# Matmul slabs set inside the delta rounds and the fourth attention, leading queries of four tiles taken as one pair, and two steps of the first two attentions reordered

## The chip, the cores and the metric

The kernel runs on one core of a Trainium2 chip. The metric is the device time in microseconds, the median of several executions. TensorE (PE) does the matmuls, VectorE (DVE), ScalarE (ACT) and GpSimd (POOL) the elementwise work, SyncE (SP) issues the DMAs.

## The reference

Four transformer layers on x (1024 features, 512 tokens). The first two belong to one model (attention with ALiBi, then neighbourhood attention, each with a cross-attention into 256 memory tokens). The last two belong to another, which sets 16 meta tokens ahead of the 512: a layer with a short convolution and a gated delta rule, and a layer with windowed attention. Each layer ends in a gated feed-forward part.

```python
# third layer
y_a = a_gate_out * causal_dwconv(a_gate_in * a_h, conv_a_w)      # the gate: 4 slabs of a_gate_out
o = gated_delta_rule(q, k, v, beta, g)                           # 4 heads, chunks of tokens
y = concat([y_a, rms_norm(o) * silu(z)]) @ w_out
# fourth layer: 16 query heads, 4 key heads, 64 features each
q, k = rms_norm(h @ wq) * d ** -0.5, rms_norm(h @ wk); v = h @ wv
pm = sink_softmax(causal(qm @ km.T), sink); om = pm @ vm         # the 16 leading (meta) queries
p = sink_softmax([qb @ km.T, banded(qb @ kband.T)], sink)        # four blocks of 128 queries
y = concat([om, p @ [vm, vband]]) @ wo
```

## The kernel before

**Slabs.** Every weight comes in slabs of 128 output features by 1024 inputs (`UP` = 8 blocks) or 1408. SP loads a slab into `raw[:, s]` (s = 0 or 1), ACT rounds it to `w_hi` (L818, `split_hi`, two halves), POOL makes `w_lo` (L606, `split_lo`, two halves). TensorE multiplies each block three times (hi·hi, hi·lo, lo·hi) by the activations, in two column halves of 264: 48 matmuls for a slab on all 528 tokens. The slot s of `w_hi` is free again when `pe_done` counts the slab before last; the accumulator `acc(s)` (PSUM banks 0, 1 or 2, 3) when DVE has read it (`acc_free[s]`). Each engine runs its own queue in the order written, and semaphores hold them together.

**First two attentions (`attend_tiles`).** Eight tiles (two heads each) of four pairs (128 queries by 256, 384 or 512 keys; tiles 6 and 7 are the memory heads). At step p TensorE does `scores(p)` (L1363), `turn(p-2)` (transposes of the probabilities, L1472) and `values(p-3)` (L1373); at the first step of a tile also `reciprocals(tile-2)` (L1490), which waits for `inv_ready` (DVE's `invert`: reciprocal and the copy L1771) and for `y_moved` (ACT's `move_y`, L1002, a copy of the tile's output out of the bank that the reciprocals then overwrite). ACT's step is `turned(p-1, h)` (L993) and `probs(p, h)` (L910) for two heads; then `y_hi(tile-2)` at pair 2 of a tile and `move_y(tile-1)` at pair 3. DVE's step is `biased` twice (L1786), `invert(tile-1)` at pair 0 and `normalise(tile-2)` at pair 1.

**Third layer.** The stage `even` ends with four slabs, the gate slabs (q0+12, q0+13; s = 0, 1), whose results DVE multiplies into `conv_y`. The stage `delta` follows: rounds -1 to 6 of five pieces i = 0 to 4. In a round, chunk r runs its levels (`first_product`, `second_products`), chunk r-1 its `tail`, chunk r+1 its `pre` work, chunk r-2 its `head`. Chunk 0 has 16 tokens, the others 128. `pre` uses banks 0 and 1, `second_products` writes bank 6. Eight slab parts of `out` stand at the end of `delta` (`slab_part`).

**Fourth attention (`attend`).** Eight tiles of five pairs: pair 0 holds the 16 leading queries, pairs 1 to 4 the four blocks of 128. Six slabs of the projection (`Hidden`, tiles 2 to 7 of q) lie in it: tile T (0 to 5) carries slab T in pairs 1, 2 and 3 (18, 18 and 12 matmuls, L1419), ahead of `values` in each step. DVE's `scaled` reads it at pair 3, ACT squares it at pair 4 (L939), TensorE sums the squares at pair 0 of the next tile (the mean square, L1406, in the same banks 4 and 5), ACT takes the logarithm and the exponential there (L944, L947), and DVE normalises at pair 1. A step p of the other work: TensorE `scores(p)` (L1363), `turn_both(p-2)` (L1396), `values(p-3)` (L1373) with the transposed reciprocals (L1437) at its end; in tiles 6 and 7 also two products of ones that nothing reads (L1435). ACT: `probs(p, 0)`, `turned_both(p-1)` (L923, L926), `probs(p, 1)`, `move_y(p-2)` (L953, waits for L1437), `y_hi(p-3)` (L958). DVE: sink column and `biased` (p), `invert(p-1)`, `normalise(p-3)` (L1761 on `y_sb`), for which `turn_both` of the next step waits. POOL stages q, k and v of each tile and makes `y_lo`. Then the stage `out` runs its 8 slabs.

Of the kernel before, what the change touches and what calls it, by code (L numbers as in the profile page):

```python
# [43 lines left out]
MIXED = 6  # L44
HEAD_TILES = (8, 9, 0, 1)
# [31 lines left out]
def plan():  # L77
# [25 lines left out]
    def att(**kw):  # L103
        add("att", **kw)
        c["pair"] += kw["nt"] * len(kw["blocks"])
        c["tile"] += kw["nt"]
        c["unit"] += kw["nt"] * len(kw["blocks"])
# [7 lines left out]
    def tail(gain, blk, layer, conv, following, mixed=False):  # L115
# [7 lines left out]
        for _ in range(FF_G):  # L123
# [15 lines left out]
    s_blocks = [dict(q=0, nq=META, keys=[(P, META)], chunks=[(0, META, 4)], bias="meta"),  # L139
                dict(q=META, nq=P, keys=[(0, KEY_STEP)], chunks=[(0, P, 0), (P, META, 4)], bias="first")]  # L140
    for b in range(1, 4):
        s_blocks.append(dict(q=META + P * b, nq=P, keys=[(KEY_STEP * (b - 1), P + KEY_STEP)],
                             chunks=[(0, P, b - 1), (KEY_STEP, P, b), (P, META, 4)], bias="band"))

# [72 lines left out]
def build(nc, d):  # L217
# [6 lines left out]
    with ctx:  # L224
# [18 lines left out]
        meta_mask = cst[0:META, o + 3 * P + 2 * META:o + 3 * P + 3 * META]  # L243
# [9 lines left out]
        neg_rows = sb("neg_rows", [P, 28])  # L253
        neg_sinks = [neg_rows[:, 0:12], neg_rows[:, 12:28]]
# [26 lines left out]
        small = region("small", 14464)  # L281
# [34 lines left out]
        v_st = small("v_st", [P, 2, 5, P])  # L316
        sq = small("sq", [P, 2, TOK], f32, 7400)
# [54 lines left out]
        def quad(k, n):  # L372

            return ps[:, k * BANK:k * BANK + DN_H * n].rearrange("p (h n) -> p h n", h=DN_H)

# [49 lines left out]
        class Chunk:  # L425

            def __init__(self, c):
                self.c, (self.t0, self.n) = c, CHUNKS[c]
                self.tok = slice(self.t0, self.t0 + self.n)
                self.levels = levels_of(c)  # L430
                self.a_t, self.x_m, self.x_t = a_ts[c % 2], x_ms[c % 2], x_ts[c % 2]
                self.state, self.next_state = states[c % 2], states[(c + 1) % 2]
                self.top, self.final = min(self.n, P // 2), "vn" if c else "vt"
                self.out_bank, self.ms_bank = 4 if c == LAST else 3, 2 if c < LAST - 1 else 5
                self.qk_t, self.erow = qk_ts[c % 3], erows[c % 3]
                self.elast = elasts[:, c % 3, :]
                self.sq4 = (slice(0, self.n), slice(None), slice(0, self.n))

            def after(self, engine, part, maker, name):

                engine.wait_ge(d_sem[part, maker], dn_at[part, maker, self.c, name])

        def rounds():

            for r in range(-1, len(CHUNKS) + 2):
                for i in range(PIECES):
# [5 lines left out]
                    yield here, mid, old, new, fin, i  # L452

        class Pair:

            def __init__(self, st, g, pos):
                self.st, self.g, self.pos = st, g, pos
                nb = len(st.blocks)  # L460
                self.b, self.slot, self.tile_slot = pos % nb, pos % 2, pos // nb
                self.c = st.blocks[self.b]
                self.nq, self.n = self.c["nq"], sum(n for _, n in self.c["keys"])
                self.tile = 2 * g + pos // nb
                self.nth = g * (2 * nb) + pos
                self.count, self.unit = self.nth + st.pair0, self.nth + st.unit0
                self.exists = self.nth >= 0
                self.q = slice(self.c["q"], self.c["q"] + self.nq)
                self.full = sum(1 for ch in self.c["chunks"] if ch[1] == P)
                self.halves = [(2 * self.nth + h) % 3 for h in range(2)]  # L470
                self.inv = (slice(0, self.nq), self.nth // 4 % 2, self.nth % 4, slice(None))

            def back(self, k):
                n = 2 * len(self.st.blocks)
                return Pair(self.st, self.g, self.pos - k) if self.pos >= k else Pair(self.st, self.g - 1, self.pos - k + n)

        def over_pairs(st, body):

            for g in range(st.nt // 2):
                for pos in range(2 * len(st.blocks)):  # L480
                    body(Pair(st, g, pos))
# [42 lines left out]
        def last_pair(st):  # L524
            return Pair(st, st.nt // 2 - 1, 2 * len(st.blocks) - 1)
# [74 lines left out]
        def _(pool):  # L600
# [32 lines left out]
            def attend(st):  # L633

                nb = len(st.blocks)
                hi_y, lo_y = outputs(st)

                def stage_q(i):
                    pool.wait_ge(s_done, (i - 1) * nb + st.pair0)
                    pool.wait_ge(tn_out, st.tn0 if i < 2 else st.tn0 + i - 1)  # L640
                    split(q_hi[:, i % 2, :], q_lo[:, i % 2, :], qk[st.h][:, st.qt + i, :], 2 * (i + st.tile0) + 2)\
                        .then_inc(qk_staged, 1)

                def stage_k(i):
                    pool.wait_ge(s_done, (i - 1) * nb + st.pair0)
                    at = i // st.group + st.kt
                    keys = qk[st.h][:, at, META:TOK].rearrange("p (b n) -> p b n", n=P)
                    meta = qk[st.h][:, at, 0:META].unsqueeze(1).to_broadcast([P, 4, META])
                    hi, lo = (k[:, i % 2, :].rearrange("p (b n) -> p b n", n=KEY_STEP) for k in (k_hi, k_lo))
                    nc.gpsimd.tensor_copy(hi[:, :, P:KEY_STEP], meta)  # L650
                    nc.gpsimd.tensor_copy(hi[:, :, 0:P], keys).then_inc(hi_staged, 1)
                    pool.wait_ge(hi_staged, 2 * (i + st.tile0) + 1)
# [3 lines left out]
                def stage_v(i):  # L656
                    pool.wait_ge(pv_done, (i - 1) * nb + st.pair0)
                    f = bass.ds((i // st.group) * P, P)
                    nc.gpsimd.tensor_copy(v_st[:, i % 2, 0:4, :], val_m[st.h][:, 0:4, f])
                    nc.gpsimd.tensor_copy(v_st[0:META, i % 2, 4, :], val_m[st.h][0:META, 4, f]).then_inc(v_staged, 1)  # L660

                def y_lo(i, b):
                    c = st.blocks[b]
                    q = slice(c["q"], c["q"] + c["nq"])
                    k = i * nb + b
                    pool.wait_ge(y_hi_ready, k + st.unit0 + 1)
                    nc.gpsimd.tensor_tensor(lo_y[:, st.y + i, q], y_sb[st.h][:, k % 2, 0:c["nq"]],
                                            hi_y[:, st.y + i, q].bitcast(f32), ALU.subtract).then_inc(y_lo_ready, 1)
                chores = [stage_k, stage_v, stage_q]
# [6 lines left out]
                for i in range(1, st.nt + 1):  # L676
                    more = Hidden(st, i) if 2 <= i < MIXED + 2 else None
                    for b in range(nb):
                        if b < 3 and i < st.nt:
                            chores[b](i)  # L680
                        if b >= 3 and more:
                            split_lo(more.q, more.s, UP, (b - 3,))
                        if b >= 3:
                            y_lo(i - 1, b - 3)
                        elif i >= 2:
                            y_lo(i - 2, b - 3 + nb)
                for b in range(nb - 3, nb):
                    y_lo(st.nt - 1, b)
# [59 lines left out]
            def delta(st):  # L748
# [8 lines left out]
                for here, mid, old, new, fin, i in rounds():  # L757
# [27 lines left out]
                    if new and i == 4:  # L785
# [4 lines left out]
                        over_heads(new.x_t[new.sq4], all_heads(ident, n), new.x_t[new.sq4], ALU.subtract, "pre")  # L790
                    if mid and mid.c == LAST and i == 2:
                        stream(st.slab0 + 2)

            for n, st in enumerate(stages):
                if st.kind == "delta":
                    stream(st.slab0)
# [11 lines left out]
        def _(act):  # L808
# [104 lines left out]
            def attend(st):  # L913

                def probs(p, h):
                    s_h = s_sb[0:p.nq, p.slot, h, 0:p.n + 1]
                    exponentials(p, h, s_h, s_h, -1.0, p_sum[p.inv][:, h:h + 1])

                def turned_both(p):
                    act.wait_ge(pt_done, 2 * p.count + 2)  # L920
                    act.wait_ge(pv_done, p.count - 1)
                    if p.full:
                        nc.scalar.activation(p_t[:, p.slot, :, 0:p.full, 0:p.nq],  # L923
                                             bank(3).rearrange("p (h c n) -> p h c n", h=2, n=P)[:, :, 0:p.full, 0:p.nq],
                                             ACT.Copy)
                    nc.scalar.activation(p_t[0:META, p.slot, :, p.full, 0:p.nq],  # L926
                                         bank(6 + p.slot)[0:META, 2 * P:4 * P].rearrange("p (h n) -> p h n", h=2)[:, :, 0:p.nq],
                                         ACT.Copy).then_inc(pt_ready[0], 1)

                def split_hidden(p):  # L930
                    if p.b in (2, 3) and 2 <= p.tile + 1 < MIXED + 2:
                        w = Hidden(st, p.tile + 1)
                        split_hi(w.q, w.s, UP, (p.b - 2,))

                def hidden(p):
                    if p.b == 4 and p.tile < MIXED:
# [3 lines left out]
                    if p.b == 0 and 0 <= p.tile - 1 < MIXED:  # L940
                        w = Hidden(st, p.tile - 1)
# [8 lines left out]
                def move_y(p):  # L950
                    act.wait_ge(pv_done, p.count + 1)
                    act.wait_ge(y_lo_ready, p.unit - 1)
                    nc.scalar.activation(y_sb[st.h][:, p.slot, 0:p.nq], bank(6 + p.slot)[:, 0:p.nq], ACT.Copy)\  # L953
                        .then_inc(y_moved, 1)

                def y_hi(p):
                    act.wait_ge(y_ready, p.unit + 1)
                    nc.scalar.activation(outputs(st)[0][:, st.y + p.tile, p.q], y_sb[st.h][:, p.slot, 0:p.nq],  # L958
                                         ACT.Copy).then_inc(y_hi_ready, 1)

                def step(p):
                    probs(p, 0)
                    hidden(p)
                    if p.back(1).exists:
                        turned_both(p.back(1))
                    probs(p, 1)
                    if p.back(2).exists:
                        move_y(p.back(2))
                    if p.back(3).exists:
                        y_hi(p.back(3))  # L970
                    split_hidden(p)
# [9 lines left out]
            def attend_tiles(st):  # L981
# [27 lines left out]
                def step(p):  # L1009
# [1372 lines left out]
```

## Time and profile before

| | us |
|---|---|
| median of 3 runs | 2696.24 (2682.99 to 2702.41) |
| the profiled execution, its own time | 2692.25 |
| its span, first to last instruction | 2690.4 |
| first attention | about 120 to 204 |
| second attention | about 742 to 854 |
| gate slabs, then delta rounds | 1423.7 to 1447.2, then to 1621.9 |
| fourth attention, its end | 2083.3 to 2265.8 |

The profile is of one execution. TensorE's busy share is high because ends of pipelined matmuls are modelled; what counts is where it waits, and at which clock it ran (PEclk: 1.00 is 2.4 GHz, 0.50 is 1.2 GHz).

### The profile page before, as it was taken

What the parts mean: (1) busy time and instruction counts of PE and PEld (TensorE: products, weight loads), DVE (VectorE), ACT (ScalarE), POOL (GpSimd) and SP (SyncE); (2) the same over time, 40 slices, a digit from 0 to 9 for tenths busy, and PEclk for the clock granted to TensorE, in tenths of its full rate; (3) what the DMA queues carried; (4) which work ended last, traced back from release to release, by engine and by line L of the source; (5) the groups of instructions that cost most, each with busy time, mean ns of one, the idle gap of its engine ahead of it and who ended that gap; (6) DMA issues with size and microseconds to landing.
All of it is one profiled execution on the core that took longest, in us unless ns stands there. A gap on an engine that the chain in (4) does not pass through costs nothing.

```text
span 2690.4 us, 45550 instructions
## 1 busy us (share of the span) xinstructions
PE 2582.8 (96%) x16250; PEld 2238.3 (83%) x16250; DVE 938.9 (35%) x1675; ACT 938.4 (35%) x1974; POOL 1180.5 (44%) x964
## 2 busy tenths in 40 slices
PE   7989999999988999999998989999999889999999
PEld 7757888888866888888997879999999667998897
DVE  3253221222153321226652444432432553442341
ACT  4274222232275322234342233222233563332231
POOL 4544444444543444444443434444444442444443
PEclk9999999999998999999997899999999897999999
DMA  4211232232320223232221002222222100223222
GB/s 166 82 34 64 93 104 88 96 108 87 107 71 17 94 94 102 86 102 95 84 79 40 1 17 87 86 96 84 93 93 73 32 25 24 87 92 102 86 99 96
DMA packets 60231, 212.89 MB, mean 79 GB/s; under 512 B 8544, under 2 KB 11232, under 8 KB 60128
## 3 DMA queue, kind: packets, MB, share of 16 engines
q1 hardware_dynamic: 60128, 211.53, 23.6%
q8 instruction: 63, 1.03, 0.2%
q14 instruction: 40, 0.33, 0.0%
HBM read 209.41 MB, written 2.10 MB: 79 GB/s over the span
## 4 chain that ended last, share of the span: by engine, by line
PE 91%; DVE 3%; ACT 3%; issue 2%; DMA 0%; DVEq 0%; POOL 0%; ACTq 0%; SPq 0%; POOLq 0%
PE ps L1249 76%; PE ps L1575 3%; PE ps L1373 2%; PE ps L1363 2%; ACT s_sb L910 1%; PE ps L1472 1%; PE ps L1419 1%; PE ps L1396 1%; PE ps L1264 1%; DVE s_sb L1786 1%; PE ps L1435 0%; DVE s_sb L1761 0%; PE ps L1490 0%; PE ps L1566 0%; ACT p_t L993 0%
## 5 line engine op out<-in xcount | busy, mean ns | idle before, releaser
L606 POOL TENSOR_TENSOR w_lo<-raw,w_hi 128x512 fp32r<-128x512 f32 (+1 forms) x704 | 976.5, 1408 | 1165.1 <-ACT w_hi L818 1164.7
L818 ACT ACTIVATE w_hi<-raw 128x512 fp32r<-128x512 f32 (+1 forms) x704 | 426.9, 653 | 1324.3 <-PE ps L1249 1302.1
L1249 PE MATMUL ps<-h_hi,w_hi 128*128 128x264 f32 (+2 forms) x2960 | 845.4, 332 | 0.1
L1249 PE MATMUL ps<-h_lo,w_hi 128*128 128x264 f32 (+2 forms) x2960 | 844.0, 332 | 0.0
L1249 PE MATMUL ps<-h_hi,w_lo 128*128 128x264 f32 (+2 forms) x2960 | 841.9, 331 | 0.0
L1249 PEld LDWEIGHTS ps<-h_hi,w_hi 128*128 128x128 f32 x2960 | 503.7, 188 | 60.1 <-issue 1.6
L1249 PEld LDWEIGHTS ps<-h_hi,w_lo 128*128 128x128 f32 x2960 | 500.5, 188 | 53.9
L1249 PEld LDWEIGHTS ps<-h_lo,w_hi 128*128 128x128 f32 x2960 | 499.7, 188 | 54.8 <-issue 1.0
L1249 PE MATMUL ps<-act_lo,w_hi 128*128 128x512 f32 (+1 forms) x880 | 280.5, 351 | 0.0
L1249 PE MATMUL ps<-act_hi,w_lo 128*128 128x512 f32 (+1 forms) x880 | 279.8, 350 | 0.0
L1249 PE MATMUL ps<-act_hi,w_hi 128*128 128x512 f32 (+1 forms) x880 | 278.8, 349 | 0.0
L1761 DVE TENSOR_TENSOR x<-x,ps 128x512 f32<-128x512 f32 (+3 forms) x96 | 66.5, 693 | 427.5 <-PE ps L1249 423.3
L1249 PEld LDWEIGHTS ps<-act_lo,w_hi 128*128 128x128 f32 x880 | 153.6, 188 | 24.0
L1249 PEld LDWEIGHTS ps<-act_hi,w_hi 128*128 128x128 f32 x880 | 153.3, 188 | 24.3
L1249 PEld LDWEIGHTS ps<-act_hi,w_lo 128*128 128x128 f32 x880 | 153.9, 188 | 22.7
L1761 DVE TENSOR_TENSOR ps<-gated,ps 128x512 f32<-128x512 f32 (+1 forms) x88 | 61.6, 701 | 168.0 <-PE ps L1249 167.7
L1756 DVE SCALAR_TENSOR_TENSOR ps<-padded,vec,ps 128x528 f32<-128x528 f32 (+1 forms) x132 | 101.2, 766 | 27.3 <-issue 16.8
L910 ACT ACTIVATE s_sb<-s_sb,n_max 128x512 f32<-128x512 f32 (+5 forms) x176 | 96.9, 550 | 12.1 <-DVE n_max L1786 12.0
L1761 DVE TENSOR_TENSOR act_lo<-ps,act_hi 128x512 f32 (+1 forms) x88 | 61.2, 696 | 104.3 <-ACT act_hi L1045 104.3
L1373 PE MATMUL ps<-p_t,v_st 128*64 128x128 f32 (+1 forms) x1136 | 95.8, 298 | 0.1
L1761 DVE TENSOR_TENSOR padded<-ps,rstd 128x528 f32<-128x528 f32 (+1 forms) x56 | 39.4, 703 | 153.9 <-PE ps L1249 142.8
L1042 ACT ACTIVATE ps<-ps 128x512 f32<-128x512 f32 (+1 forms) x88 | 51.4, 584 | 107.1 <-DVE ps L1756 107.1
(269 smaller groups left out, 2543.0 us busy)
## 6 DMA issues: line engine op xcount, KB each, us to landing
raw<-slabs_d SPq DMA_DIRECT2D x288, 512.0 KB, 3.3
raw<-slabs_d SPq DMA_DIRECT2D x64, 704.0 KB, 4.0
bias_sb<-rpb_d SPq DMA_DIRECT2D x6, 896.0 KB, 5.2
bias_sb<-alibi_d SPq DMA_DIRECT2D x6, 384.0 KB, 3.2
x<-x_d SPq DMA_DIRECT2D x1, 2048.0 KB, 13.1
out_d<-x SPq DMA_DIRECT2D x8, 256.0 KB, 4.5
mem_in<-mem_d SPq DMA_DIRECT2D x1, 1024.0 KB, 7.2
dn_cst<-dn_consts_d SPq DMA_DIRECT2D x1, 512.0 KB, 4.6
```

Source lines behind the costliest of these rows:

```text
L606: nc.gpsimd.tensor_tensor(w_lo[:, s, a * P:b * P], raw[:, s, a * P:b * P], w_hi[:, s, a * P:b * P].bitcast(f32), ALU.subtract).then_inc(lo ...
L818: nc.scalar.activation(w_hi[:, s, a * P:b * P], raw[:, s, a * P:b * P], ACT.Copy)\
L910: nc.scalar.activation(out, src, ACT.Exp, bias=n_max[0:out.shape[0], p.slot, h:h + 1], scale=sign, accum_out=total).then_inc(p_ready, 1)
L1042: nc.scalar.activation(acc(2, st.used), acc(2, st.used), ACT.Silu).then_inc(silu_ready, 1)
L1249: last = nc.tensor.matmul(ps[:, s * 2 * BANK + po:s * 2 * BANK + po + n], w[:, s, wk], a[:, k, to:to + n], start=(k == 0 and w is w_hi and ...
L1264: last = nc.tensor.matmul(out, a[:, k, t0:t0 + n], w[:, s, wk], start=(k == 0 and w is w_hi and a is hi), stop=(k == DT - 1 and w is w_lo))
L1363: last = nc.tensor.matmul(bank(p.halves[h])[0:p.c["nq"], col:col + n], a[hp, p.tile_slot, p.q], b[hp, p.tile_slot, k0:k0 + n], start=(b is ...
L1373: last = nc.tensor.matmul(out[HD * h:HD * h + HD, :], v_st[0:n, p.tile_slot, vb, HD * h:HD * h + HD], p_t[0:n, p.slot, h, j, 0:p.c["nq"]], ...
L1396: last = nc.tensor.transpose(to, s_sb[0:p.nq, p.slot, h, 1 + col:1 + col + n], ident[0:p.nq, 0:p.nq])
L1575: last = nc.tensor.matmul(out[:, h, :], lhs(h), rhs(h), start=True, stop=True)
L1756: return nc.vector.scalar_tensor_tensor(*a, **kw)
L1761: return nc.vector.tensor_tensor(*a, **kw)
```

## The change

**First two attentions:** ACT's `move_y` goes from pair 3 to pair 2 and `y_hi` from pair 2 to pair 3; DVE's `invert` from pair 0 to pair 2.

**Delta:** of the four gate slabs only the first stays in `even`. The other three lie in the rounds, in parts (`GATE_PARTS`), ahead of `second_products`. `pre` takes banks 6 and 7 for chunks 0 and 1, and chunk 0's `second_products` bank 1. `pre`'s two products of round piece 1 and 2 both stand at piece 2, ACT's first exponentials at piece 1. ACT and POOL split the later slabs inside the rounds.

**Fourth attention:** a list `ORDER` of 34 pairs takes the place of 8 times 5: pairs 0 to 3 of each tile, and two pairs (tile, 4), which hold the leading queries of four tiles (4 times 32 rows of a staged copy `qm_hi`), one after (3, 3), one after (7, 0). k and v are staged once per group of four tiles. The slab of a tile lies in pairs 0, 1, 2 (12, 18, 18 matmuls), at pair 0 behind `values`; squares at pair 2's and logarithm at pair 3's end of ACT's step, the mean square at the end of TensorE's step at pair 3 of the same tile. The first slab of `out` is begun at pairs (6, 0), (6, 2), (7, 0), (7, 2), six matmuls each, and ended behind the last pair (24).

```diff
+ORDER = [(t, b) for t in range(TILES) for b in range(4)]
+ORDER.insert(ORDER.index((7, 0)) + 1, (7, 4))
+ORDER.insert(ORDER.index((3, 3)) + 1, (3, 4))
+FIRST_OUT = {(6, 0): 0, (6, 2): 1, (7, 0): 2, (7, 2): 3}
+        GATE_PARTS = {(-1, 0): (12, 1, range(4)), (-1, 1): (12, 1, range(4, 8)), (-1, 2): (13, 0, range(3)),
+                      (-1, 3): (13, 0, range(3, 6)), (-1, 4): (13, 0, range(6, 8)), (0, 0): (13, 1, range(3)),
+                      (0, 1): (13, 1, range(3, 6)), (0, 2): (13, 1, range(6, 8))}
 # POOL, delta
+                    if r == -1 and i in (0, 3):
+                        split_lo(st.slab0 // 2 - 1, i // 3, UP)
 # ACT, attend: at the end of a step
+                def hidden(p):
+                    if p.b in (0, 1) and 2 <= p.tile + 1 < MIXED + 2:
+                        split_hi(w.q, w.s, UP, (p.b,))
+                    if p.b == 2 and p.tile < MIXED:
                         nc.scalar.activation(head_sq[:, w.s, :], qk[st.h][:, w.tile, :], ACT.Square)
+                    if p.b == 3 and p.tile < MIXED:
                         act.wait_ge(tn_ms, w.tn + 1)
                         nc.scalar.activation(halves_of(head_root[:, w.s, :], 2), split_acc, ACT.Ln, ...)
 # ACT, attend_tiles
-                    if p.b == 3 and p.after(4):
+                    if p.b == 2 and p.after(4):
                         move_y(p.tile - 1, 1 - p.tile_slot)
-                    if p.b == 2 and p.after(8):
+                    if p.b == 3 and p.after(8):
                         y_hi(p.tile - 2, p.tile_slot)
 # ACT, end of even and delta
-                for i in (13, 14):
-                    for s in range(RING):
-                        split_hi(q0 + i, s)
+                split_hi(q0 + 13, 0)
+                early_hi = {(-1, 2): (q0 - 1, 1), (0, 1): (q0, 0), (0, 4): (q0, 1)}
 # TensorE, attend
                 def step(p):
                     scores(p)
+                    if p.nth >= 2:
                         turn_both(p.back(2))
-                    hidden(p)
+                    if p.b:
+                        hidden(p)
+                    if p.nth >= 3:
                         values(p.back(3))
+                    if p.b == 0:
+                        hidden(p)
+                    mean_square(p)
+                    if (p.tile, p.b) in FIRST_OUT:
+                        first_out(st, FIRST_OUT[p.tile, p.b])
 ...
+                pe.wait_ge(y_lo_ready, st.unit0 + len(ORDER))
+                for k in range(4, DT):
+                    first_out(st, k)
+            def first_out(st, k):
+                q, (hi, lo) = (st.slab0 + MIXED) // 2, outputs(st)
+                if k == 0:
+                    begin(q, 0)
+                    pe.wait_ge(tn_rt, st.tn0 + MIXED)
+                if k < 4:
+                    pe.wait_ge(y_lo_ready, st.unit0 + ORDER.index((3, 4)) + 1)
 # TensorE, end of even, delta, out
-                many(q0 + 12, 2, 2, hi, lo)
+                slab(q0 + 12, 0, 2, hi, lo)
+                    if (r, i) in GATE_PARTS:
+                        q, s, parts = GATE_PARTS[r, i]
+                        for k in parts:
+                            slab_part(st, st.slab0 // 2 - 14 + q, s, k)
-                    many(q0, DT // 2, st.blk, *outputs(st))
+                    slab(q0, 1, st.blk, *outputs(st))
+                    many(q0 + 1, DT // 2 - 1, st.blk, *outputs(st))
 # DVE, attend_tiles
-                        if p.b == 0 and p.tile >= 1:
+                        if p.b == 2 and p.tile >= 1:
                             invert(p.tile - 1, 1 - p.tile_slot)
 # DVE, delta
+                gates = {(-1, 2): 1, (0, 0): 2, (0, 3): 3}
```

## Rows read from the trace of the kernel before

**Rows 1.** The page: the span, and the chain that ended last by engine.
```profile
span 2690.4 us, 45550 instructions
...
PE 91%; DVE 3%; ACT 3%; issue 2%; DMA 0%; DVEq 0%; POOL 0%; ACTq 0%; SPq 0%; POOLq 0%
```

**Rows 2.** L1490's waits in 140:172, 172:204, 765:800, 800:856 us (total, times).
```profile
  ACT y_tile L1002: 4.1, 3
...
  ACT y_tile L1002: 3.6, 3
...
  ACT y_tile L1002: 5.1, 3
...
  ACT y_tile L1002: 6.4, 5
```

**Rows 3.** Stretches of one tile: us, busy of PE, PEld, DVE, ACT, POOL, clock.
```profile
153.02:163.67 10.65, 9.07 (x89) 6.38 (x89) 6.45 (x24) 8.27 (x26) 5.61 (x7) 1.00 0.16 47
...
795.51:809.61 14.10, 12.41 (x124) 9.21 (x125) 7.67 (x20) 10.90 (x26) 5.86 (x7) 1.00 0.18 75
```

**Rows 4.** Chain of waits, second attention: start, us, what.
```profile
780.78 0.50 ACT y_tile L1002
...
781.41 0.63 PE ps L1490 x4
```

**Rows 5.** Timeline: DVE's copy of `invert` in each of the two attentions.
```profile
152.70 0.44 DVE L1771 COPY p_rec<-p_inv 128x512 f32<-128x512 f32 x1
...
781.09 1.18 DVE L1771 COPY p_rec<-p_inv 128x512 f32<-128x512 f32 x1
```

**Rows 6.** Chain of waits, gate slabs and delta rounds -1 and 0.
```profile
1423.69 23.48 PE ps L1249 x192
...
1454.50 0.39 PE ps L1575 x8
...
1465.74 1.06 PE ps L1580 x4
...
1470.10 1.24 POOL a_lv L752
...
1472.07 2.05 PE ps L1575 x8
```

**Rows 7.** A stretch of the delta rounds, columns as in rows 3.
```profile
1455.70:1478.20 22.50, 16.22 (x106) 12.99 (x103) 4.04 (x11) 4.46 (x10) 6.94 (x7) 0.50 0.00 1
```

**Rows 8.** Chain of waits, a tile of the fourth attention.
```profile
2165.53 0.86 PE ps L1396 x6
...
2169.30 0.85 PE ps L1396 x6
2170.14 0.89 PE ps L1406 x4
2171.04 0.95 PE ps L1373 x12
```

**Rows 9.** Timeline of ScalarE there.
```profile
2166.41 0.60 ACT L923 ACTIVATE p_t<-ps 128x512 f32<-128x512 f32 x1 [0.40 <-PE ps L1396]
...
2167.68 0.25 ACT L953 ACTIVATE y_sb<-ps 128x128 f32<-128x128 f32 x1
...
2168.96 0.63 ACT L939 ACTIVATE head_sq<-qk 128x528 f32<-128x528 f32 x1
...
2172.46 0.30 ACT L958 ACTIVATE ym_hi<-y_sb 128x128 fp32r<-128x128 f32 x1
...
2172.95 0.68 ACT L944 ACTIVATE head_root<-ps,vec 128x528 f32<-128x528 f32 x1
```

**Rows 10.** Fourth attention: tile 2, tile 5, then tiles 6 and 7 before the drain.
```profile
2126.25:2149.45 23.20, 20.71 (x161) 15.88 (x160) 11.20 (x42) 12.65 (x44) 9.56 (x15) 0.85 0.07 24
...
2190.81:2211.47 20.66, 17.88 (x160) 13.79 (x160) 10.51 (x42) 12.54 (x44) 9.59 (x15) 1.00 0.08 27
2211.47:2251.54 40.07, 37.04 (x216) 25.03 (x215) 16.21 (x73) 19.70 (x74) 11.33 (x19) 0.59 0.08 28
```

More of the change, by code:

```diff
@@ L316, in build @@
         v_st = small("v_st", [P, 2, 5, P])
+        qm_hi, qm_lo = (small(n, [P, TILES, META_Q], f32r) for n in ("qm_hi", "qm_lo"))
         sq = small("sq", [P, 2, TOK], f32, 7400)
@@ L477, in over_pairs, with into, y @@
+            def into(self, t):
+                if self.meta:
+                    return t[:, self.st.y + 4 * self.group:self.st.y + 4 * self.group + 4, 0:META]
+                return t[:, self.st.y + self.tile, self.q]
+            def y(self):
+                y = y_sb[self.st.h][:, self.slot, :]
+                return y.rearrange("p (t n) -> p t n", n=META_Q)[:, :, 0:META] if self.meta else y
         def over_pairs(st, body):
-            for g in range(st.nt // 2):
-                for pos in range(2 * len(st.blocks)):
-                    body(Pair(st, g, pos))
+            for nth in range(len(ORDER)):
+                body(Pair(st, nth))
@@ L675, in attend, with step @@
                 stream(st.slab0 + 2)
[L676 to L688, printed above, removed]
+                def step(p):
+                    more = Hidden(st, p.tile + 1) if 2 <= p.tile + 1 < MIXED + 2 else None
+                    if p.tile == 2 and p.b == 0:
+                        stage_k(1)
+                    if p.tile == 2 and p.b == 2:
+                        stage_v(1)
+                    if p.b == 1 and p.tile + 1 < TILES:
+                        stage_q(p.tile + 1)
+                    if p.b in (2, 3) and more:
+                        split_lo(more.q, more.s, UP, (p.b - 2,))
+                    if p.nth >= 3:
+                        y_lo(p.back(3))
+                over_pairs(st, step)
+                for k in (2, 1, 0):
+                    y_lo(last_pair(st).back(k))
                 streamed(st.slab0 + MIXED + 2)
@@ L755, in all_heads @@
                     return m[0:n, 0:n].unsqueeze(1).to_broadcast([n, DN_H, n])
-                for here, mid, old, new, fin, i in rounds():
+                for r, here, mid, old, new, fin, i in rounds():
                     if here:
@@ L1677, in pre @@
                         k.after(pe, "pre", "pool", "xt")
-                        turn(quad(1, n)[0:n], lambda h: k.x_t[0:n, h, 0:n], n).then_inc(done, 1)
-                for s in range(RING):
-                    pe.wait_ge(acc_free[s], st.slab0 // 2)
-                for here, mid, old, new, fin, i in rounds():
+                        turn(quad(k.pre1, n)[0:n], lambda h: k.x_t[0:n, h, 0:n], n).then_inc(done, 1)
+                for r, here, mid, old, new, fin, i in rounds():
+                    if r == 1 and i == 0:
+                        for s in range(RING):
+                            pe.wait_ge(acc_free[s], st.slab0 // 2)
                     if here:
@@ L1970, in step @@
                         stt(tile, tile, q_gain, head_root[:, w.s, :], ALU.mult, ALU.mult).then_inc(tn_out, 1)
+                for t in range(4):
+                    rows = slice(META_Q * t, META_Q * t + META_Q)
+                    copy(meta_sinks[rows, :, :],
+                         neg_sinks[1][rows, :].rearrange("p (g t h) -> p g t h", g=2, h=2)[:, :, t, :])
                 over_pairs(st, step)
@@ L2238, in delta @@
                 ts(neg_ident[:, :], ident, -1.0, None, ALU.mult).then_inc(gate_made, 1)
-                for here, mid, old, new, fin, i in rounds():
+                gates = {(-1, 2): 1, (0, 0): 2, (0, 3): 3}
+                for r, here, mid, old, new, fin, i in rounds():
+                    if (r, i) in gates:
+                        second_gate(st.slab0 - 4, gates[r, i])
                     if here:
```

315 lines of the change are left out of this document (166 added, 149 removed).

## The prediction

> **What bounds the kernel now.** The page comes first: the chain that ended last runs on TensorE for 91% of a span of 2690.4 us [rows 1]. So time is won only where TensorE waits, runs at the lower clock, or does less. I looked for such places with the page's slices, then took the chain of waits and the busy time by stretch for the three stages that the change touches.
>
> In the first two attentions TensorE stands still once in each tile, ahead of L1490, until ScalarE has moved a tile's output: 4.1 us for three tiles, then 3.6, 5.1 for three, and 6.4 for five [rows 2], 19.2 us for fourteen. In a tile of the second attention that is plain: the move starts at 780.78, at the end of ScalarE's pair 3 [rows 4], and TensorE had come to L1490 well before. ScalarE itself is busy 8.27 of 10.65 us in a tile of the first attention and 10.90 of 14.10 in one of the second [rows 3].
>
> Between the gate slabs and round 1 of delta TensorE has little to do and long chains to wait for. The four gate slabs take 23.48 us from 1423.69 on, and round 1 begins at 1472.07 [rows 6]: 24.9 us for two rounds of small products, most of them at the 1.2 GHz level, where the stretch 1455.7 to 1478.2 stands [rows 7].
>
> In the fourth attention a tile of five pairs takes 20.66 us, one with part of its time at the lower clock 23.20, and tiles 6 and 7, which carry no slab, 40.07 for nine steps at a mean clock of 0.59 [rows 10]. A step without a slab takes 3.77 us from one turn to the next (2165.53 to 2169.30), though TensorE's own work in it is less: it waits for VectorE's biases, reciprocals and normalising [rows 8].
>
> **The change, part by part.**
>
> *A, move_y a pair sooner.* It removes or adds no instruction. The move's input is there: the last values of tile T-1 are made in TensorE's step (T, 2), and ScalarE's step (T, 2) ends a step later, since it needs TensorE's turn of (T, 3). The move then ends one step (about 2.7 to 2.9 us) sooner, more than any wait of 1.2 to 1.7 us, so the wait goes. Twelve of the sixteen waits lie in the loops; from rows 2 they are 7.7 in the first attention, 5.1 for three of the second, and about 3.9 for its last three: 16.7 us. What is late next: ScalarE. In the second attention it has 14.10 - 10.90 = 3.2 us free in a tile, and 1.6 when the tile shrinks by 1.6, so the gain is nearly whole: 6 times 1.4 = 8.4. In the first it has 2.4 free, 1.1 after a shrink of 1.3, and it trades values with TensorE twice in a pair; I take 1.0 of 1.3, 6.0 in all. `invert` moves to pair 2, where TensorE no longer stands still while VectorE makes it: 0.2 + 1.18 us in the second attention [rows 5]. VectorE's step there is 1.75 us of biases, so 3.1 against a step of 2.94; 0.2 us late, which ScalarE's buffer (it takes the maxima half a microsecond after they are there) hides. If it doesn't, 12 times 0.2 = 2.4 are lost; I take half. A: 8.4 + 6.0 - 1.2 = 13. Bounds: 17 (all waits gone), 4 (ScalarE sets the tile, and only a third goes).
>
> The copy of `invert` takes 0.44 us in one attention and 1.18 in the other, where GpSimd's split of q runs beside it [rows 5]. The Trainium skill (GPSIMD Engine Reference, section 1, Specifications) says that GpSimd shares its SBUF interfaces with VectorE, with contention when VectorE's instruction runs in a two-port mode or has two SBUF inputs. By it the copy stays slow wherever it meets a staging, and `y_hi` a pair later pushes GpSimd's staging a pair later too, to just where `invert` now stands. Were the whole 0.74 us on the path in every tile of both attentions, A would be 4 rather than 13; the later bias has the slack named above, so I don't take it.
>
> *B, three gate slabs into the rounds.* Each is 23.48 / 4 = 5.87 us [rows 6], work that stays. Before, from the end of the first gate slab (1423.69 + 5.87 = 1429.56) to round 1: 1472.07 - 1429.56 = 42.5 us. After: round -1 holds two slabs (11.7) and its own small products (2.1 us, an estimate: some twenty of 16 tokens); the chain of chunk 0 (gate row, differences, exponentials, a, its turn) took at most 7.3 us alone, from the slabs' end at 1447.17 to round 0 at 1454.50 [rows 6], and fits between the parts. I add 0.7 for the last wait, for x_m. Round 0: one slab (5.9), its own products, some 6 us at 2.4 GHz (an estimate: what is left of 1472.07 - 1454.50 = 17.6 without the 5.3 below is 12.3 us of products at 1.2 GHz [rows 7] and short waits), and 0.5 for a_m. What stays is the chain behind the last turn, with no slab part beside it: from 1466.80 (end of the turn at 1465.74) to 1472.07, ACT's copy, GpSimd's three products of 1.24 to 1.26 each [rows 6], 5.3 us. Sum 14.5 + 5.9 + 6.5 + 5.3 = 32.2, so 10.3 less. Moved with it: ScalarE's splits, two in round 0 of 1.2 us, at pieces 1 and 4; at piece 4 it falls behind a_t, into GpSimd's 2.5 us, so it is hidden. GpSimd's split of slab (13, 1) takes 2.6 us at piece 3 of round -1 ahead of chunk 0's x_t; TensorE has 2.2 + 1.5 us of slab parts there, which cover it; if not, 1 to 2 us are lost. SP's loads come free by `lo_done` as before. VectorE gets one 0.7 us product at each of three pieces, not on a path. Round 1 still begins after some 5 us of thin work, so its half-clock products (the stretch to 1478.2, rows 7) are left as they are. B: 10, bounds 5 and 12.5.
>
> *C, the fourth attention.* The new tile has TensorE's work of four pairs. Pieces by rows 8, and 0.122 us per slab matmul from rows 6: four turns 3.2 us, values with their reciprocal's transpose 4.6, scores 2.4, mean square 0.9, slab 5.9: 17.0. But the change makes TensorE wait twice for ScalarE in each tile, where it did not. The mean square of tile T now stands in step (T, 3), and its square comes at the end of ScalarE's step (T, 2), behind `move_y`, which itself waits for the values of that very step. ScalarE starts after a turn at 2166.41, its `y_sb` 1.27 later, then `y_hi` (0.2 until the next may start), then 0.63 of square, 2.3 us in all [rows 9]; TensorE has 1.2 us of values to do meanwhile. So it waits 1.1. At pair 0 the slab stands behind the values and needs the logarithm (0.68), again behind `move_y` and `y_hi`: 1.15 more. With two waits of 0.25 for the normalised values where the slab precedes them, the tile is 17.0 + 2.3 + 0.5 = 19.8; by adding the four steps turn to turn I get 5.3 + 5.2 + 5.1 + 4.6 = 20.2. I take 20.2, against 20.66: 0.45 less, 2.3 for tiles 1 to 5. The pair (3, 4) costs a step of 3.77 less the logarithm's wait that it hides: -2.6. The first tile has a step less, 3.3 less about 0.8 for four copies of sinks: 2.5. Tiles 6 and 7: eight steps for nine; at the mean of 40.07 / 9 = 4.45 that is 4.4 less, but the first wait for the logarithm (1.1) and 24 matmuls of `out` (2.9 at the higher clock) come in: about 0.5. In return `out` has 24 matmuls less: 2.9. GpSimd's six stagings less free VectorE's small ops a little: 1. C: 2.3 - 2.6 + 2.5 + 0.5 + 2.9 + 1 = 6.6, say 7. Bounds: -5, if each of five tiles falls to the lower clock as tile 2 did (2.5 us more [rows 10]); 17, if tiles 6 and 7 keep the higher one (step 4.1 for 4.45 and up to 7 us with the slab pieces).
>
> Sum: 13 + 10 + 7 = 30; 2692.25 - 30 = 2662. The profiled execution lies 4 us under the median of the three runs, 2696.24; I set the time at 2664. What a measurement here can tell from no change is about 1%.
>
> **The rivals.**
>
> R1, ScalarE sets the tile in the first two attentions. For it: 8.27 of 10.65 us [rows 3]. Against: it stands idle for some 1.9 us straight after each move. A is then 4: 2673.
>
> R2, the two new waits bring the lower clock into tiles 0 to 5. For it: tile 2 shows it with about 2.9 us of waits [rows 10], and the new tile has as much, and its slabless stretch is near 10 us. Against: tiles 3 to 5 had the same and kept 1.00. Five times 2.5: 2676.
>
> R3, the higher clock holds through tiles 6 and 7, since `out` pieces stand where there was none: 8 to 10 more, 2655.
>
> R4, the gate slabs don't hide: `second_products` of chunk 0 stand behind each part, and the chain of the round grows by the part's length. For it: parts are ahead of the products that others wait for. B is 1: 2673.
>
> R5, slower than before: the 1.2 GHz level through all of tiles 0 to 5. At half the clock 17.0 us of work become up to 34, 14 more than the tile's 20.2, 83 in all, 2747. It decides from the third such tile on, some 60 to 80 us of lower clock more than before; the page shows no such stretch with slabs in it.
>
> **How the numbers follow.** Forecast 0.49 (its own range 2654 to 2673), R1 0.16, R2 0.16, R3 0.12, R4 0.04, R5 0.03. The range takes in R1, R2, R3 and their sums: 2643 to 2686. Faster by over 1% means under 2669: four fifths of the forecast, R3, a little of R1 and R2, 0.54. Slower is R5, 0.03. The rest 0.43.
>
> **What would show it.** In the profile after: L1490's wait for y_tile falls from 1.3 to under 0.3 us in the loops, and a tile of the second attention from 14.10 to 12.6. Round 1 of delta begins 32 us after the first gate slab ends. In the fourth attention L1406 waits for head_sq and L1419 at pair 0 for head_root, 1.1 us each, and the tile takes 20.2. Wrong it would be if the tile takes 18.5 or less (ScalarE is ahead of what I think) or over 22 (the clock).

## The result, and the profile after

The changed kernel takes 2650.14 us (median of four, 2646.16 to 2656.01), the kernel before beside it 2694.81: a ratio of 0.985, interval 0.9816 to 0.9885, some 45 us gained. The forecast was 2664, some 30 us of gain. 2650 lies in the stated range (2643 to 2686), but not in the range that I gave the forecast itself (2654 to 2673), and the parts are not what I forecast: two brought about twice as much, one nothing.

The page after: the span and the chain by engine, for [rows 1].
```profile
span 2654.2 us, 45186 instructions
...
PE 93%; DVE 3%; ACT 2%; issue 1%; DMA 0%; POOL 0%; DVEq 0%; SPq 0%; ACTq 0%; POOLq 0%
```

**First two attentions.** L1554 is the L1490 of before. What it waited for in both attentions together, then one tile of each (columns as in rows 3), then a stretch of the chain of waits in the second:
```profile
  ACT y_tile L1028: 1.9, 2
```
```profile
162.33:171.77 9.44, 9.09 (x89) 6.39 (x90) 7.38 (x23) 8.39 (x27) 5.51 (x6) 1.00 0.43 153
786.42:798.79 12.37, 12.37 (x125) 9.19 (x126) 7.08 (x20) 10.93 (x27) 5.53 (x6) 1.00 0.35 137
```
```profile
786.42 0.58 PE ps L1554 x4
787.00 0.90 PE ps L1390 x6
787.90 1.02 PE ps L1536 x8
788.93 1.03 PE ps L1411 x16
...
798.79 0.26 PE ps L1554
```
The wait of over a microsecond a tile [rows 2] is gone; in sixteen tiles one of 0.9 us is left twice. In the second attention TensorE is busy 12.37 of 12.37 us, where it was 12.41 of 14.10 [rows 3]; chain pieces follow one another with no idle time. The second attention took 111.8 us from its first pair to its last normalised tile before (742.4 to 854.2) and 99.4 after (738.4 to 837.9). By the same measure the first went from 92.1 to 83.9; up to the start of the second, 6.9 of these 8.2 us are left (620.4 and 613.5 us from the first pair of the one to that of the other). Together 12.4 + 6.9 = 19.3, forecast 13.

**Delta.** The chain of waits through rounds -1 and 0, for [rows 6]:
```profile
1414.32 2.92 PE ps L1630 x24
...
1441.70 0.67 PE ps L1644 x4
1442.37 0.02 issue
1442.39 0.61 ACT a_t L1191
...
1444.41 1.27 POOL x_t L779
...
1445.82 1.10 PE ps L1644 x4
...
1447.80 0.55 PE ps L1639
```
The first gate slab ends at 1414.32, round 1 begins at 1447.80: 33.5 us, forecast 32.2, before 42.5. So 9.0 of the 10.3. But rounds 1 to 6 shrank too, from 149.8 us (1472.1 to 1621.9) to 136.6 (1447.8 to 1584.4): 13.2 more, of which the prediction says nothing. Half of that is idle time of TensorE (15.8 us, then 9.2), half its own work (134.0 us, then 127.4, the same matmuls at a higher mean clock). One of these rounds, before and after, with both (the clock is the column after POOL):
```profile
1506.70:1539.00 32.30, 29.57 (x217) 28.32 (x217) 13.23 (x22) 8.88 (x20) 13.43 (x12) 0.86 0.01 1
```
```profile
1479.20:1507.80 28.60, 27.84 (x216) 26.76 (x217) 13.76 (x22) 8.95 (x20) 13.36 (x11) 0.91 0.01 1
```

**Fourth attention.** Distances from one mean square to the next (L1458, before L1406) are the tile's period. Here are the stretches of one tile, of most of the next (its mean square comes at 2138.4), and of tiles 6 and 7 with what of tile 5 follows its mean square, for [rows 10]:
```profile
2091.18:2112.89 21.71, 18.69 (x147) 14.24 (x147) 10.57 (x32) 11.54 (x38) 10.06 (x17) 0.92 0.08 25
2112.89:2136.20 23.31, 21.64 (x141) 16.69 (x141) 8.24 (x32) 9.31 (x31) 5.52 (x9) 0.71 0.08 25
...
2184.73:2233.81 49.08, 42.42 (x317) 29.74 (x317) 20.52 (x81) 25.77 (x90) 11.68 (x20) 0.86 0.07 23
```
TensorE's waits there (total, times, longest), and ScalarE's queue ahead of a mean square, where the square comes last, behind both moves, for [rows 9]:
```profile
PE ps L1458 <- ACT head_sq L967: 7.8, 6, 1.3
...
PE ps L1447 <- ACT head_root L972: 5.0, 4, 1.3
```
```profile
2110.58 0.60 ACT L953 ACTIVATE p_t<-ps 128x512 f32<-128x512 f32 x1
...
2111.85 0.25 ACT L981 ACTIVATE y_sb<-ps 128x128 f32<-128x128 f32 x1
2112.01 0.29 ACT L986 ACTIVATE ym_hi<-y_sb 128x128 fp32r<-128x128 f32 x1
2112.21 0.63 ACT L967 ACTIVATE head_sq<-qk 128x528 f32<-128x528 f32 x1
```
The two new waits are there, and about as long as foretold (1.3 us each, forecast 1.1; the second stands in four tiles). But the mean squares start at 2067.9, 2091.2, 2112.9, 2138.4, 2163.0 and 2184.7: a tile takes 21.7 to 25.5 us, 23.4 on average, not 20.2. That is over the 22 that the prediction names as its sign of being wrong. The same mean square in windows of 2 us:
```profile
2110.00:2112.00 2.00, 1.54 (x14) 0.77 (x12) 1.77 (x2) 1.87 (x7) 1.98 (x3) 1.00 0.00 0
2112.00:2114.00 2.00, 1.11 (x3) 0.91 (x4) 1.52 (x6) 1.34 (x5) 1.62 (x2) 0.67 0.00 0
2114.00:2116.00 2.00, 2.00 (x10) 1.19 (x9) 0.43 (x2) 0.00 (x0) 0.06 (x1) 0.50 0.37 84
...
2124.00:2126.00 2.00, 2.00 (x13) 1.59 (x12) 0.00 (x0) 0.00 (x0) 0.00 (x0) 0.50 0.00 0
2126.00:2128.00 2.00, 2.00 (x17) 2.00 (x16) 1.18 (x5) 1.25 (x4) 0.00 (x0) 0.92 0.00 0
```
The engine waits, the granted clock goes from 2.4 to 1.2 GHz (1.00 to 0.50) with it, and stays there for some 12 us. From a mean square just ahead of the attention (2062.0 before, 2023.8 after) to the end of the span the kernel before took 628.4 us and this one 630.4: part C brought nothing. These 2 us are the sum of larger parts: 1.4 more up to the first mean square in the attention (42.7 us, then 44.1), 11.0 more from there to the last one (107.3, then 118.3), and 10.4 less behind it (478.4, then 468.0).

### The profile page after: what moved, and what is told of

Its sections match the earlier page's. It is cut to its first block, busy times and chain, and to the rows that moved or that the text cites. A ratio compares the mean times of both kernels' runs of the same rounds, so it can differ in the third digit from the quotient of the medians.

```text
span 2654.2 us, 45186 instructions
## 1 busy us (share of the span) xinstructions
PE 2569.6 (97%) x16168; PEld 2223.2 (84%) x16168; DVE 941.2 (35%) x1631; ACT 933.4 (35%) x1932; POOL 1161.7 (44%) x938
## 4 chain that ended last, share of the span: by engine, by line
PE 93%; DVE 3%; ACT 2%; issue 1%; DMA 0%; POOL 0%; DVEq 0%; SPq 0%; ACTq 0%; POOLq 0%
PE ps L1276 76%; PE ps L1639 3%; PE ps L1411 2%; PE ps L1447 1%; PE ps L1536 1%; PE ps L1390 1%; PE ps L1432 1%; PE ps L1630 1%; ACT s_sb L940 1%; PE ps L1291 1%; DVE s_sb L1856 1%; PE ps L1403 1%; DMA mem_in<-mem_d 0%; PE ps L1458 0%; PE ps L1300 0%
## 5 line engine op out<-in xcount | busy, mean ns | idle before, releaser
L1276 PE MATMUL ps<-h_hi,w_hi 128*128 128x512 f32 (+2 forms) x2912 | 839.3, 334 | 0.1
L1276 PE MATMUL ps<-h_lo,w_hi 128*128 128x512 f32 (+2 forms) x2912 | 833.5, 332 | 0.0
L1276 PE MATMUL ps<-h_hi,w_lo 128*128 128x512 f32 (+2 forms) x2912 | 833.0, 332 | 0.0
L1276 PEld LDWEIGHTS ps<-h_hi,w_hi 128*128 128x128 f32 x2912 | 494.7, 188 | 59.8 <-issue 1.6
L1276 PEld LDWEIGHTS ps<-h_lo,w_hi 128*128 128x128 f32 x2912 | 494.2, 188 | 56.9 <-issue 1.0
L1276 PEld LDWEIGHTS ps<-h_hi,w_lo 128*128 128x128 f32 x2912 | 493.3, 188 | 55.4
L1276 PEld LDWEIGHTS ps<-act_hi,w_lo 128*128 128x128 f32 x880 | 153.8, 188 | 23.7
```

Source lines behind the costliest of these rows:

```text
L1276: last = nc.tensor.matmul(ps[:, s * 2 * BANK + po:s * 2 * BANK + po + n], w[:, s, wk], a[:, k, to:to + n], start=(k == 0 and w is w_hi and ...
```

## The experiments

The kernel before ran beside each; its median was 2694.25 beside runs 1, 4, 6 and 7, 2693.32 beside 8 to 11, and 2693.49 beside 2, 3, 5 and 12. Times are medians, brackets are intervals of the ratio; 0.001 is 2.7 us.

**1. The values' move alone** (kernel before and part A):
```
-  if p.b == 3 and p.after(4): move_y(...)      + if p.b == 2 ...
-  if p.b == 2 and p.after(8): y_hi(...)        + if p.b == 3 ...
-  if p.b == 0 and p.tile >= 1: invert(...)     + if p.b == 2 ...
```


> The kernel before with the first two attentions' reordering alone (move_y at pair 2, y_hi at pair 3, invert at pair 2). Theory, from the trace after (first attention about 7 us shorter, second 12.4): 17 to 21 us faster than before, ratio 0.992 to 0.994. Rival (the stages end earlier but ScalarE gives it back later, or the difference is the run's): 5 us or less, ratio 0.998 or more.

2670.6 us, 0.9915 [0.989, 0.994]: 23.6 less. Its second attention ends at 835.9 by the trace, 18.3 before that of the kernel before; a further 3.1 lie between there and the last head mean square of delta (751.9 us for 755.0), where the code is the same, so the trace's stages are good to about 3 us.

**2 and 3. A's two halves**, each alone on the kernel before: the first two lines of that diff, and the third.

> The kernel before with the order of move_y and y_hi alone, invert left at pair 0. Theory (TensorE stood still until the move, so the move carries the gain): 14 to 22 us less than before, the waits of L1490 for y_tile gone. Rival (the moved invert carries a good part, since VectorE's reciprocals stand between two scores): at most 10 us.

> The kernel before with invert at pair 2 alone, move_y and y_hi left. Theory: the wait for the move stays, 0 to 5 us less than before. Rival: 10 us or more.

The move alone: 2672.11, 0.992 [0.9904, 0.9936], 21.4 less. `invert` alone: 2694.57, 1.0008 [0.9996, 1.002], nothing. Waits of L1490 in the two attentions with `invert` alone, then with the move alone:
```profile
PE ps L1490 <- ACT y_tile L1002: 20.9, 15, 1.7
```
```profile
PE ps L1490 <- ACT y_tile L1002: 1.9, 2, 0.9
```
So the gain is the wait for the move; `invert` adds nothing that these intervals can tell (21.4 without it, 23.6 with it). The copy in `invert`, 1.18 us in the tile of [rows 5], took over a microsecond in three of the sixteen tiles of before only; I had read one and took it for all. With the move alone none is slow:
```profile
L1771 DVE COPY p_rec<-p_inv x16: 426/427/428, 137.2 to 837.0; 128x512 f32<-128x512 f32 x16
```

**4. The order of a chunk's preparation alone** (kernel before; ScalarE's exponential of the gate row from piece 0 to 1, and with it TensorE's products that overwrite its input, from 1 to 2):
```
 def pre(k, i):      # ScalarE           def pre(k, i):      # TensorE
-    if i == 0:  (erow, elast)          -    if i == 1:  (keys by keys)
+    if i == 1:                         +    if i == 2:
```


> The kernel before, with only the order of pre in the delta rounds changed: ScalarE's two first exponentials of the next chunk at piece 1 instead of 0, TensorE's product of k with k at piece 2 instead of 1. No slab is moved. Theory (in round pieces 0 and 1 ScalarE's copy of z stood behind an exponential that waits for VectorE's tail work): rounds 1 to 4 shorter by 3 to 5 us each, 11 to 15 us in all, ratio 0.9945 to 0.996. Rival (rounds 1 to 4 are shorter after because the slab parts ahead of them leave TensorE at the higher clock): 3 us or less, ratio 0.999.

2674.58, 0.9927 [0.9898, 0.9956]: 19.7 less, more than expected. By the trace the stretch from the last normalised tile to the last head mean square took 739.3 us for 755.0: 15.7 less, 14.4 of it behind the start of round 1 (122.8 for 137.1). 3.3 more lie in the fourth attention, which is untouched (104.0 us for 107.3 from first to last mean square), so they are no effect of the edit. What ScalarE and TensorE waited for in rounds 1 to 3 of the kernel before:
```profile
ACT erow L1160 <- DVE dlast L1761: 24.8, 3, 9.1
...
PEld ps L1575 <- ACT z_m L1140: 8.7, 5, 2.6
...
PE ps L1575 <- ACT z_m L1140: 7.5, 5, 2.3
```
and with the order alone (PEld is TensorE's weight load):
```profile
PEld ps L1574 <- ACT z_m L1140: 2.0, 3, 0.9
PE ps L1574 <- ACT z_m L1140: 1.4, 2, 0.7
```
ScalarE, in order, stood up to 9.1 us at `erow` for VectorE's differences, with `z_m`, which the next level's products need, behind it. TensorE's wait for `z_m` falls from 7.5 to 1.4 us in all (PEld's 8.7 and 2.0 are the same waits, counted ahead of the weight load). That is most of what its idle time loses from round 1 on, 13.6 to 6.9 us. The other 7.7 of the 14.4 are its own work: 901 matmuls in 123.6 us at a mean clock of 0.90 before, 902 in 115.8 at 0.96 here. So more than half of the gain is the clock that no longer falls behind those waits.

**5. TensorE's half of that order alone** (kernel before; products at piece 2, `erow` left):

> The kernel before with the first products of the preparation of a chunk (L1664) a piece later on TensorE, ScalarE's exponential of the gate row left at piece 0. Theory (ScalarE's place for that exponential, ahead of z_m of piece 1, made the chain): 0 to 3 us less than before. Rival (it was TensorE that waited at piece 1 for the exponential, ahead of the next level's product): 10 us or more.

2688.84, 0.9984 [0.9972, 0.9997]: 4.7 less, a little over the range of the theory and far from its rival; the 8.7 and 7.5 us of waits for `z_m` stand unchanged in its trace. So ScalarE's place carries most of the gain, with the products moved along. (Its half alone was not tried: the products would overwrite what `erow` reads.)

**6. The changed kernel with the old order put back:**

> The changed kernel with only the order of pre put back (exponentials at piece 0, the product of k with k at piece 1), slab parts still in the rounds. Theory: 10 to 15 us slower than the changed kernel, ratio to before 0.989 to 0.991; round 1 still begins about 33 us after the first gate slab. Rival (the clock): within 3 us of the changed kernel, 0.985.

2662.09, 0.9882 [0.9857, 0.9908], 12.0 more than the changed kernel. The same stretch takes 747.2 us, for 735.4 in the changed kernel, and `erow` again waits 24.6 us for `dlast`. With the old order and the gate slabs 747.2, without either 755.0 (751.9 in run 1): the slabs bring 5 to 8, the order 11.8 on top. The two act in different places. Round 1 begins 34.0 us after the first gate slab, as in the changed kernel (33.5); from there on the rounds take 136.9 us at a clock of 0.90, as in the kernel before (137.1 at 0.90) and not 125.5. So the slabs ahead of the rounds do nothing for their clock, which was run 4's rival.

**7. A and B without C:**

> The changed kernel without its fourth attention: before plus the reordering of the first two attentions plus everything in delta. Theory (the new fourth attention costs 2 us): 39 to 43 us faster than before, ratio 0.984 to 0.9855, level with the changed kernel or 1 to 3 us faster than it. Rival (the fourth attention brings the forecast 7 us): 30 to 34 us faster, ratio 0.9875.

2648.74, 0.9837 [0.9809, 0.9866]: 1.4 below the changed kernel, which is no difference; the rival's 0.9875 lies outside the interval. C brings nothing, so the next runs take it apart.

**8. ScalarE's square and root sooner** (changed kernel; these two stood there in the kernel before, and the change moved them to the end of the pair; the split stays at the end):
```
 def step(p):
     probs(p, 0)
+    hidden(p)          # square, logarithm and exponential
     turned_both(p.back(1)); probs(p, 1); move_y(p.back(2)); y_hi(p.back(3))
-    hidden(p)
+    split_hidden(p)
```


> The changed kernel with ScalarE's square and root of the hidden head norm ahead of the turned copies in a pair, the split left where it is. Theory (the two waits of 1.3 to 1.5 us in each of tiles 0 to 5 stand because those two instructions are issued behind the moves of the values): the waits of L1458 and L1447 for ScalarE fall from 9.0 and 5.0 us to under 1 us each, the granted clock no longer drops at a mean square, the distance of mean squares falls from 21.7 to 23.6 us to 20 to 21, and the time is 8 to 15 us below the changed kernel. Rival (the tile is held by VectorE's scores and the low clock that the many narrow steps bring, the waits only fill it): the waits go, the distance stays above 21.5, at most 3 us are gained.

2633.61, 0.977 [0.9751, 0.9789]: 18.5 below the changed kernel run beside it (10.), past the theory's end. Both waits are gone. First mean square to the last, in the kernel before, the changed one, and this one:
```profile
2104.70:2212.00 107.30, 93.68 (x800) 72.09 (x799) 53.66 (x213) 63.30 (x221) 47.92 (x75) 0.96 0.06 21
```
```profile
2067.90:2186.20 118.30, 104.31 (x746) 79.14 (x747) 52.49 (x179) 59.35 (x194) 36.52 (x57) 0.83 0.06 19
```
```profile
2063.80:2159.80 96.00, 88.50 (x748) 68.76 (x747) 50.32 (x179) 58.35 (x193) 34.94 (x55) 0.96 0.07 23
```
Of the 22.3 us between the last two, TensorE's waits are 6.5 (14.0 less 7.5) and 15.8 are its own work, the same matmuls at a mean clock of 0.83 against 0.96. So the two waits of 1.3 us cost 22.3 / 5 = 4.5 us a tile, and 15.8 of the 22.3 is clock. Of the idle time only 6.5 goes, though the two waits were 12.8, since TensorE then waits more for the normalised values (9.8 us from 2050 to 2200, for 2.8 in run 10). A tile is 19.2 us, for 21.5 before and 23.7 in the changed kernel.

**9. Sinks of the leading queries made at the start:**
```
 ts(neg_rows[:, :], rows[:, 0:28], -1.0, None, ALU.mult)
+for t in range(4): copy(meta_sinks[...], neg_sinks[1][...])      # and not ahead of over_pairs
```


> The changed kernel with the four copies of the leading queries' sinks made once at the start of the kernel, in place of in front of the fourth attention. Theory (the copy took 5.07 us beside GpSimd's pass and held the first pair): 3 to 5 us less. Rival (the next VectorE operation meets the same GpSimd pass and takes the delay): 0 to 1 us.

2647.6, 0.9822 [0.9804, 0.984], 4.5 less. VectorE at the start of the attention, in the changed kernel and in this one:
```profile
2048.09 6.23 DVE L1841 COPY meta_sinks<-neg_rows 32x4 f32<-32x4 f32 x4
2054.39 0.47 DVE L1831 TENSOR_TENSOR s_sb<-neg_rows 128x2 f32<-128x2 f32 x1
```
```profile
2050.04 4.07 DVE L1831 TENSOR_TENSOR s_sb<-neg_rows 128x2 f32<-128x2 f32 x1
```
The rival's mechanism is real: the next small operation took the delay (4.07 us for two columns). But by then the first pair's biases were made, and the delay no longer holds the start: from the mean square ahead of the attention to the first one in it 39.5 us, for 44.1. The times of this run and of run 10 alone would not tell (their intervals overlap), but runs 8 and 11, which differ by the same edit, show it again: 42.9 and 38.2 us.

**10. The changed kernel again, and 11. both edits:**

> The changed kernel once more, on the same chip as the three edits of it: 0.985 of the kernel before (0.982 to 0.989), a gain of 36 to 48 us.

> The two edits before together. Theory: the gains add, 10 to 18 us below the changed kernel. Rival: at most 4 us.

The changed kernel: 2652.08, 0.9836 [0.9817, 0.9856]. Both edits: 2623.5, 0.9741 [0.9721, 0.9761], 28.6 less than it and 70 less than the kernel before, the fastest version here. That is 5.6 more than the two gains summed; the trace has 5.3 of it behind the last mean square, where this run kept the higher clock and the one with ScalarE's edit alone did not (below). That it kept it because of the sinks was not shown.

**12. Both edits, no piece of `out` inside the attention:**
```
-FIRST_OUT = {(6, 0): 0, (6, 2): 1, (7, 0): 2, (7, 2): 3}
+FIRST_OUT = {}                      # all eight pieces behind the last pair
```


> The kernel with both edits (ScalarE's square and root sooner, sinks at the start), with the eight pieces of out slab 0 after the last pair, none in tiles 6 and 7. Theory (the pieces keep TensorE busy enough there that the granted clock stays at 1.00): the clock falls to 0.50 in tiles 6 and 7, 8 to 14 us more than with them. Rival (the pieces only fill waits and cost what they cost after the attention): within 3 us.

2630.85, 0.9771 [0.9753, 0.9789]: 7.4 more, between the two. The 25 us behind the last mean square with both edits, then without the pieces, then with the pieces but the sinks in their old place (run 8):
```profile
2153.60:2178.60 25.00, 20.83 (x188) 14.78 (x188) 14.19 (x54) 16.36 (x58) 9.11 (x14) 1.00 0.13 44
```
```profile
2152.20:2177.20 25.00, 20.57 (x138) 13.88 (x137) 12.53 (x46) 14.35 (x50) 8.64 (x13) 0.71 0.13 43
```
```profile
2159.80:2184.80 25.00, 21.49 (x155) 15.64 (x154) 12.52 (x46) 14.34 (x50) 8.65 (x13) 0.80 0.14 44
```
Without the pieces the clock falls, as the theory has it; but it falls in run 8 too, which has them. In the same 25 us it stands at 0.76 in the changed kernel, 0.80 in run 10 and 0.93 in runs 6 and 9, all with the pieces. They are worth about 7 us where the clock then holds, and don't ensure it. What does is open.

## Why the prediction was right and wrong

The gain was forecast as 13 + 10 + 7 = 30 us and came out as 44.7. By the runs A is 23.6 (run 1), B 21.9 (run 7 less run 1), C -1.4 (run 7), each good to some 7 us or worse by the intervals. A and B are too small by 10.6 and 11.9, C too large by 8.4. That the time still lies in the range is luck: with C as forecast it would be some 2642, outside it.

**A: mechanism right, its size off.** The wait went, and a tile of the second attention takes 12.37 (forecast 12.6). The mis-sized terms: "6 times 1.4 = 8.4" for the second attention, where the stage lost 12.4 us, 1.7 a tile in seven tiles; the 1.2 taken off for `invert`, which costs nothing (run 1 against run 2); 6.0 for the first, measured 6.9. The bound of 17, called "all waits gone", left out the waits outside the loops, though rows 2 alone add up to 19.2. R1 is refuted where it counted: in the second attention TensorE has no idle time left and ScalarE 1.4 us of 12.37. In the first, TensorE stands 0.35 of 9.44 us still; over both attentions its waits for ScalarE's probabilities grew from 8.0 to 12.0 us. From a statement of the Trainium skill (GPSIMD Engine Reference, section 1, Specifications) I had worked out that the copy of `invert` would stay slow, and that A might be 4. That did not come, and doesn't refute the statement: in the changed kernel no copy takes over 0.61 us, and at 781.52 it has GpSimd's copy of the values beside it and not its subtraction, as the 1.18 us one of before had. In the kernel before the slow copies cost nothing, since the wait for the move covered them: in run 3 none in the second attention takes over 0.43 us, and nothing is gained. Small operations held up beside GpSimd's are seen in run 9.

**B: right at the slabs, blind behind them.** 33.5 us for 32.2 forecast; R4 is refuted. The failed step is a missing one: "Round 1 still begins after some 5 us of thin work, so its half-clock products ... are left as they are" treated the rounds as unchanged, while the diff moved `erow` and the products a piece later. The chain of waits of before has the place in plain rows; I listed what the change adds to ScalarE's queue and not what it takes from the front of it. It is worth 11.8 (run 6) to 15.7 us (run 4), over half of it at the higher clock in run 4.

**C: wrong sign of a term, by R2.** By stretch, the forecast had 2.5 us gained up to the first mean square, 0.3 lost to the last one (2.3 for the tiles less 2.6 for the pair) and 4.4 gained behind it; the trace has 1.4 lost, 11.0 lost and 10.4 gained. The two waits were foretold with place and length, and costed at 2.3 us a tile of idle time. The step that failed is the argument against R2: "tiles 3 to 5 had the same and kept 1.00". Also, the 20.66 that the new tile was set against is a tile at the full clock; the five of before take 21.5 on average. Run 8 gives the two waits' whole price, 18.5 us, or 22.3 by the trace for five tiles, over two thirds of that clock. R2's own price, 2.5 a tile, was near the 3.2 that the rows give (15.8 / 5). The sinks' four copies, which I had at 0.8 us, took 6.23 and cost some 4.5 (run 9). R3, whose 2655 is the nearest time, came in part: of the 50 us behind the last mean square the changed kernel has the first half at 0.76 and the second at 1.00, the kernel before 0.64 and 0.68. What of the 10.4 us gained there is clock, and what is fewer steps and products, no run separates. R5 did not come. With both repaired C is worth 2648.74 - 2623.5 = 25 us, more than my bound of 17.

## What to carry to other kernels

A short wait on TensorE, in a stretch of small products, is to be priced with the clock that falls behind it: here two of 1.3 us a tile cost 4.5 us a tile, over two thirds of it at the lower clock, and in the delta rounds the same holds for more than half of what shorter waits gave back. When a diff changes an order in an in-order queue, read for each instruction both what now stands ahead of it and what no longer does: the largest gain of B and the loss in C's tiles were instructions put behind or ahead of others on ScalarE. And when a total comes out near the forecast, run the parts alone before believing the reasons; here it led to a version that is 28.6 us faster.

## What the hardware showed that I had not expected

The engine's busy share does not tell its clock. Over the five tiles TensorE was busy 88% of the time in the changed kernel at 0.83 (104.3 of 118.3), and 87% in the kernel before at 0.96 (93.7 of 107.3); with the two waits of 1.3 us taken out it is busy 92% (88.5 of 96.0) at 0.96 (run 8). The share is itself raised by a low clock, since the same matmuls then last longer: 104.3 us for 88.5.

A tiny VectorE operation can last as long as several of GpSimd's. One copy of 32x4 took 5.07 us, where its neighbours took 0.16 and 0.18:
```profile
2048.76 5.07 DVE meta_sinks L1841
...
2053.90 0.16 DVE meta_sinks L1841
```
and it ended, at 2053.83, with GpSimd's four passes of 128x512 beside it (2053.80):
```profile
2048.86 4.94 POOL L629 TENSOR_TENSOR w_lo<-raw,w_hi 128x512 fp32r<-128x512 f32 x4
```
The Trainium skill (GPSIMD Engine Reference, section 1, Specifications) names the shared SBUF interfaces; the measured delay is that of all four passes, not of one. It is seen three times: the 4.07 us of run 9 ended at 2054.11 with passes that ended at 2054.09, and run 11 has 4.06 us. Not every VectorE operation is held: in run 9 the bias of 128x144 that starts at 2049.57, inside the same passes, took 0.37 us, as the one ahead of it did.
